# The six raw tail sets of an expert unit placed behind the first gate/up row of its main rows

## What is computed

```python
def expert_block(args):
    e, tok = args
    xb = xpad[tok]
    gu = xb @ w_gu[e] + b_gu[e]
    g, up = jnp.split(gu, 2, axis=-1)
    g = jnp.minimum(g, SWIGLU_LIMIT)
    up = jnp.clip(up, -SWIGLU_LIMIT, SWIGLU_LIMIT)
    glu = g * jax.nn.sigmoid(g * SWIGLU_ALPHA)
    return ((up + 1.0) * glu) @ w_down[e] + b_down[e]
```

## Time and profile before

| | us |
|---|---|
| median of 3 runs | 1828.2 |
| the 3 runs | 1827.42 to 1828.77 |
| profiled execution, its own time | 1831.0 |
| span of its profile | 1829.0 |
| PE busy (matmuls) | 1702.5 |
| DVE busy | 1327.4 |
| ACT busy | 1090.6 |
| DMA, mean rate over the span | 266 GB/s |

### The profile page before, as it was taken

One profiled execution on the slowest core, in us unless ns is written; L12 is line 12 of the kernel. 1 busy time (PEld: TensorE's weight loads), 2 busy tenths in 40 slices (PEclk: granted clock), 3 DMA queues, 4 the chain that ended last, 5 costly groups with the idle time before them and its releaser, 6 DMA issues.

```text
span 1829.0 us, 29152 instructions
## 1 busy us (share of the span) xinstructions
PE 1702.5 (93%) x8545; PEld 1260.4 (69%) x8546; DVE 1327.4 (73%) x1137; ACT 1090.6 (60%) x1043; POOL 530.6 (29%) x376
## 2 busy tenths in 40 slices
PE   5989969967999999999999999999999999999896
PEld 4766658855578677888877887678667577666583
DVE  6487753557679696989978898769667677674685
ACT  5234263426468575778767786667666666664573
POOL 5233140333132161522323322126222225221250
PEclk9999979977999999999999999999999999999898
DMA  8210102238788798999998998789868789777674
GB/s 265 86 35 24 74 31 93 105 139 325 266 324 340 289 341 320 378 391 394 380 335 336 380 391 325 272 325 374 338 242 291 278 321 326 280 263 254 239 272 188
DMA packets 114072, 485.85 MB, mean 266 GB/s; under 512 B 16319, under 2 KB 28929, under 8 KB 81249
## 3 DMA queue, kind: packets, MB, share of 16 engines
q1 hardware_dynamic: 96016, 445.58, 63.1%
q0 software_dynamic: 18000, 39.49, 8.7%
HBM read 451.79 MB, written 33.23 MB: 265 GB/s over the span
## 4 chain that ended last, share of the span: by engine, by line
PE 57%; DMA 6%; DVE 6%; issue 4%; ACT 2%; SPq 1%; POOLq 0%; DVEq 0%; ACTq 0%; POOL 0%
PE ps L1594 16%; PE ps L1596 15%; PE ps L1595 15%; DMA raw_weights<-in_w_down 5%; PE ps L1609 5%; DVE w_lo L1442 4%; PE ps L1647 3%; ACT w_hi L1298 2%; PE ps L1567 1%; PE ps L1617 1%; DMA raw_more<-in_final_norm_g 1%; SPq L1173 1%; PE ps L1671 1%; DVE raw_weights L1556 1%; DVE raw_weights L1544 1%
## 5 line engine op out<-in xcount | busy, mean ns | idle before, releaser
L1442 DVE TENSOR_TENSOR w_lo<-raw_weights,w_hi 128x2048 fp32r<-128x2048 f32 x256 | 577.1, 2284 | 145.8 <-ACT w_hi L1298 145.7
L1298 ACT ACTIVATE w_hi<-raw_weights 128x2048 fp32r<-128x2048 f32 x256 | 485.7, 1911 | 226.1 <-PE ps L1596 118.6
L1594 PE MATMUL ps<-w_hi,xT 128*128 128x512 f32 x1024 | 414.7, 405 | 9.2 <-issue 7.7
L1595 PE MATMUL ps<-w_lo,xT 128*128 128x512 f32 x1024 | 402.3, 393 | 0.0
L1596 PE MATMUL ps<-w_hi,xT 128*128 128x512 f32 x1024 | 401.8, 392 | 0.0
L1442 DVE TENSOR_TENSOR w_lo<-raw_more,w_hi 128x2048 fp32r<-128x2048 f32 x128 | 290.0, 2285 | 28.3 <-ACT w_hi L1298 28.2
L1224 POOL DMA_INDIRECT x_rows<-h_rows,next_list x33 | 80.2, 2432 | 615.2 <-issue 615.2
L1594 PEld LDWEIGHTS ps<-w_hi,xT 128*128 128x128 f32 x1024 | 193.8, 189 | 88.4 <-issue 48.5
L1298 ACT ACTIVATE w_hi<-raw_more 128x2048 fp32r<-128x2048 f32 x128 | 244.1, 1908 | 0.1
L1596 PEld LDWEIGHTS ps<-w_hi,xT 128*128 128x128 f32 x1024 | 193.7, 189 | 42.6
L1595 PEld LDWEIGHTS ps<-w_lo,xT 128*128 128x128 f32 x1024 | 194.2, 190 | 36.8
(11 more groups left out here) (294 smaller groups left out, 2238.0 us busy)
## 6 DMA issues: line engine op xcount, KB each, us to landing
raw_weights<-in_w_gu SPq DMA_DIRECT2D x192, 1024.0 KB, 8.2
raw_more<-in_w_gu SPq DMA_DIRECT2D x64, 1024.0 KB, 6.8
raw_weights<-in_w_down SPq DMA_DIRECT2D x64, 1024.0 KB, 9.8
raw_more<-in_w_down SPq DMA_DIRECT2D x64, 1024.0 KB, 12.2
rows<-in_x SPq DMA_DIRECT2D x12, 512.0 KB, 5.6
w_in_sb<-in_w_in SPq DMA_DIRECT2D x12, 512.0 KB, 4.2
raw_weights<-in_w_out SPq DMA_DIRECT2D x1, 4096.0 KB, 13.4
acc_rows<-region_c SPq DMA_DIRECT2D x8, 512.0 KB, 2.7
```

The costliest lines, as they stand in the source:

```text
L1298: S.activation(w_hi[:, j % RING, :], raw(j % RING), ACT.Copy).then_inc(hi_done, 1)
L1442: V.tensor_tensor(w_lo[:, j % RING, :], raw(j % RING), w_hi[:, j % RING, :].bitcast(F32), ALU.subtract).then_inc(lo_done, 1)
L1594: T.matmul(out, hi, hi_w, start=first, stop=False)
L1595: T.matmul(out, hi, lo_w, start=False, stop=False)
```

## The change

In units with a tail the waits for `bias_done` and `y_tail_folded`, the tail's bias and the raw sets 0 to 5 move from the head of the unit to the place behind main row 0. The wait for `xT_tail_done` stays at the head. The tail's transposes move from behind row 3 to behind row 4. Nothing is added or removed, and no other engine's program changes.

```diff
--- before.py
+++ after.py
@@ -1652,18 +1652,19 @@
                 def unit(t):
                     if t:
                         pe.wait_ge(xT_tail_done, u + 1)
-                        pe.wait_ge(bias_done, u + 1)
-                        pe.wait_ge(y_tail_folded, u + 1)
-                        for g in range(t):
-                            T.matmul(ps[:, BANK_TAIL + g, :], pick[:, 1, :], bias[:, :], start=True, stop=False)
-                        for k in range(RING):
-                            gate_up_tail(k, t)
                     pe.wait_ge(xT_lo_done, 2 * u + 2)
                     for k in range(KT - LAST):
                         pe.wait_ge(lo_done, NP * u + k + 1)
                         for b in range(4):
                             last = gate_up(b, k)
                         last.then_inc(mm_done, 1)
+                        if k == 0 and t:
+                            pe.wait_ge(bias_done, u + 1)
+                            pe.wait_ge(y_tail_folded, u + 1)
+                            for g in range(t):
+                                T.matmul(ps[:, BANK_TAIL + g, :], pick[:, 1, :], bias[:, :], start=True, stop=False)
+                            for j in range(RING):
+                                gate_up_tail(j, t)
                         if k == 1:
                             pe.wait_ge(bias_done, u + 1)
                             for b in range(4):
@@ -1676,7 +1677,7 @@
                         if k == 2 and t:
                             for j in range(RING, KT):
                                 gate_up_tail(j, t)
-                        if k == 3 and t:
+                        if k == 4 and t:
                             transpose_h_tail(t)
                     pe.wait_ge(lo_done, NP * u + KT)
                     for b in range(4):
```

## The result

The change makes the kernel faster. Its median is **1813.33 us** over 4 runs (1811.18 to 1814.90), that of before in the same comparison 1828.05 us (1827.42 to 1828.77): a ratio of 0.9907, with an interval of 0.9892 to 0.9923, which is 14.1 to 19.7 us (the medians are 14.7 apart). The profiled execution took 1812.91 us of its own.

The account below looks back on a forecast made before the run. PE's own stream, busy 93% of the span, was taken to set the end. The terms -5.6 - 8.4 + 4.3 + 0.5 = -9.2 us, from the median of 1828.2, gave 1819.0 us, range 1814 to 1825.

Parts of the forecast that it names:

- The wait for the last tail's sum: Tail's bias at the head of four units whose predecessor had a tail: row 0 covers the wait, -5.6 us.
- The "issue" waits: Tail's bias in two units, 7.2 us with no semaphore behind them in the profile: left as they are, 0.
- The transposes behind row 4: Tail's transposes in six units whose predecessor had no tail: PE arrives 2.73 us later, covering their waits, -8.4 us.
- How far the landing moves: Loads of pieces 6 to 11, issued 2.73 us later: piece 7 lands 0.7 of that later, 1.9 us.
- waits of set 7: New wait of set 7 for piece 7: about 0.1 us in three units, 1.3 in three, +4.3 us in all.
- +0.5 of transposes: Tail's transposes, still a little late in the three units where piece 7 lands earlier: +0.5 us over the six.
- the addition: POOL's addition of the last unit's rows in HBM, from +2.28: done earlier when loads stand back, the reason for 0.7.
- The rival in which piece 7 lands in time and both waits go: Piece 7 lands as before or in time, since loads beside the addition only shared its time: 1814.2 us, chance 0.12.
- The price of a wait: Waits at the tail's bias and transposes counted at the idle time the profile shows: 5.6 and 8.4 us.
- The slower rival: Landing shifts over 3.1 us, chance 0.10, half slower; at 3.5, three clock drops after set 7's waits, 1.7 each: 1833.
- The two groups: Split of piece 7 in the six units before the change: three at 13.8 us in the mean, three at 15.1.

Follow-up runs that it names:

- the run beside its parts: The changed kernel measured once more, beside runs of the sets' move alone and the transposes' move alone: 1815.18 us, ratio 0.9919 to the kernel before.
- Behind row 1: The changed kernel with the tail's bias and sets 0 to 5 behind main row 1 instead of row 0: 1846.41 us, ratio 1.0089 to the kernel before.
- the addition held back: POOL's addition of main rows in HBM held until the next unit's gate/up pieces are split: kernel before 1819.68 us, changed 1812.79, sets behind row 1 1813.81.

## Why the prediction was wrong in size

**The wait for the last tail's sum: right.** -5.6 was forecast for four units, and they are gone. The "issue" waits stayed, as forecast.

**The transposes behind row 4: right.** -8.4, and no L1624 wait is left.

**How far the landing moves: the step that failed.** The prediction said "With 0.7 the landing moves by 1.9 us", and from that +4.3 us of waits of set 7 and +0.5 of transposes. The landing moved by 0.68 in the unit at 680, and over the six units with a plain predecessor the mean of the splits of piece 7 went from +14.4 to +14.9; none is later than +15.13, and set 7's part starts at +15.66. Both terms are 0. The 0.7 was read from one unit as a constant share. The runs show two parts in its place: nearly nothing for the first 2.7 us, and nearly all of what comes after. I had named the addition as what the loads make way for. The runs clear it of this: it holds the loads in the change as it did before, by 2.3 to 2.6 us in the unit at 680. What the delay lets pass is the gather, which the prediction left out. The rival in which piece 7 lands in time and both waits go, 1814.2 us, is what happened; it had 0.12, and its reason, the addition, was the wrong one too.

**The price of a wait: too small.** The sum took waits as the profile shows them, 14.0 us. The unit at 680 can be measured from head to head. This is the next head in the kernel before, and the last matmul before the tail's bias of the earlier trace rows:

```profile
728.50 0.39 PE L1594 MATMUL ps<-w_hi,xT 128*128 128x512 f32 x1
...
1181.99 0.39 PE L1596 MATMUL ps<-w_hi,hT 128*128 128x512 f32 x1
```

Before, 680.02 to 728.50 is 48.48 us; after, 677.40 to 724.65 is 47.25. The unit became 1.23 shorter for a wait of 1.04. The reason is how the gap is drawn: matmuls start every 0.23 us and are drawn 0.39 long. The one at 1181.99 would have been followed at 1182.22; the bias started at 1183.79, a delay of 1.57, where the profile shows 1.41. Measured so, from head to head, the units in which the ten waits vanished are 15.9 us shorter together, 0.19 more for each wait than the 14.0 drawn. In the second profile of the change, that of the run beside its parts, it is 16.0. Both lie inside the measured 14.1 to 19.7.

**The sum made anew:** -5.6 - 8.4 - 1.9 + 0 = -15.9 us, against -9.2 forecast. From 1828.2 that is 1812.3, where 1813.3 was measured. Of the 6.7 us that the sum missed, 4.8 are the wait that didn't come and 1.9 the price of a wait.

**The slower rival** was right as a mechanism but lies one row further on. Behind row 1 set 7 did wait, for 18.9 us in 12 waits, and the granted clock fell. It is 16.3 us slower than before though both old waits are gone, worth 15.9 as worked out above: 32.2 us of loss. The new waits are 21.2 of it (18.9 and 12 times 0.19), and 11 are left for the stretches at the lower clock. The trace bears this out: the granted clock stands at 0.50 for 23.8 us in all around five of the waits (from 700, 963, 1209, 1482 and 1618 us), which costs 11.9 us at most, since PE waits in a small part of it. I had priced three such stretches at 1.7 each.

**The two groups.** Three of the six units had piece 7 a good 1 us later than the other three before the change; after it the two groups are the same. The three are those whose successor has a tail, and there POOL gathers that tail's 32 rows as well (L1230, `x_tail`), behind the main rows. From issue to landing this second gather takes, in the unit at 1132 before and at 1130 in the change's second profile:

```profile
x_tail<-h_rows,next_tail POOLq DMA_INDIRECT x1, 8.1
```

```profile
x_tail<-h_rows,next_tail POOLq DMA_INDIRECT x1, 3.9
```

It is issued 1.2 us behind the head before, so it runs among the loads and lands at +9.3; in the change it lands at +4.8, when the loads have only just been issued. The groups differ with the addition held back too (+12.3 to +12.9 against +11.4 to +11.7), and not in the change with the addition held back (+11.9 to +12.2 in both). So this goes with the gather as well; no run moved the second gather alone.

## What to carry to other kernels

Before pricing a delayed load at a share of its delay, list each transfer that runs beside it and when that ends: here delay was free while it let one of them pass, and nearly full price after that, so the step from free to costly was a single row. Test the two halves of a reordering as one, since the first half alone may only move the wait to a place that the second half covers. And price a wait of TensorE by the distance between starts, not by the idle time drawn.

## What the hardware did that I had not expected

- **An indirect transfer slows the loads by more than its own bytes.** The gather and the addition move 128 rows of 4 KB each, 0.52 MB, which at 400 GB/s are 1.3 us. They cost the two loads 2.4 us and 2.3 to 3.3 us, at DMA shares that are nearly full either way, and the gather does so at least in part when its own packets are over. Moving the addition by some 14 us within the unit (from +2.3 to +16.7) was worth 10 us in the order of before.
- **Of two waits of nearly the same length one cost the clock and one didn't.** After the wait of 2.48 us ahead of 1207.39 in the kernel behind row 1 the granted clock was 0.58 from 1209 to 1213; after one of 2.17 ahead of 1568.37 it was 1.00 up to 1573. The Trainium skill (TensorE: Matmul & The Clock Gate, Part 1) has the clock at half rate after idleness; the first agrees and the second doesn't, so the length of the wait alone doesn't tell.
